# Two layers of an encoder as one block, with the seam between them, the launch and the last store rewritten

## The chip, the cores and the metric

The kernel runs on one core of a Trainium2 chip. The metric is the device time of one execution in microseconds. TensorE (PE) multiplies, VectorE (DVE) and ScalarE (ACT) do the elementwise work, GpSimd (POOL) and SyncE (SP) mostly issue transfers.

## The reference, cut to what matters

Two sequences (256 and 512 tokens, width 1024, float32) pass through the same two layers. They are held together as 768 tokens, six tiles of 128. A layer is:

```
xn   = rms_norm(x, norm1_g)
proj = xn @ w_in          # 9616 columns: q/k/v of A (3 groups x 6 heads x 64),
                          # conv/v/o/gates of B, q/k/v of C, 3 x 1024 branch gates
A: dilated window attention, q and k normed per head and rotated, 3 groups merged
B: bidirectional mLSTM, 4 heads of 128
C: differential attention, 4 heads
x  = x + (sigmoid(g0)*yA + sigmoid(g1)*yB + sigmoid(g2)*yC) @ w_out
hg, hu = rms_norm(x, norm2_g) @ w_ffn_in          # 2 x 2816 columns
x  = x + (silu(hg) * hu) @ w_ffn_out
```

Every product is made of three passes: weights and activations are split into a high part (rounded to the matmul's format) and the low rest, and high x high, high x low and low x high are added up.

## The kernel before, in words

**Programs.** Each engine has its own instruction stream, and they meet on semaphores. There are three blocks. A small first one has SP load x tile 0 and the identity (L712, L713), POOL the other five x tiles, the rotary table and the masks (L717 to L721), and VectorE set `eps`. Then `nc.Fori(0, DEPTH)` (L727) runs the layer block twice, and after each turn clears all semaphores behind a barrier (L2147 to L2151), so that waits can count from zero. The last block stores y in two transfers (L2156, L2157). Every block ends with a barrier of all engines.

**Order in the layer block.** A list, STEPS (`schedule()`, L339), is walked by every engine, each doing its part of each step: `rms` (the square sum and root on ScalarE, then the scaled row on VectorE), `norm` (eight transposes on TensorE, the high copy `xh` on ScalarE, the low rest `xl` on VectorE), `first` (splits of the first eight weight sub-blocks), `piece c t` (chunk c of w_in times token tile t, 24 matmuls, three banks of PSUM in turn), and behind them the steps of attention, mLSTM, gates and branches. In-order engines make this list the order of all work.

**Weights.** SP loads sub-blocks of up to 512 KB into a ring of three (`wraw`, RAW = 3); a load waits on `w_lo`, the count of splits that VectorE has finished. ScalarE makes `wh` from it (L1139, L1368), VectorE `wl` (L1428, L1769). `wh` and `wl` have two halves of four sub-blocks, one per chunk in turn. SPLITS (L420) hangs the splits of chunk c on the steps of chunk c-1 that come after chunk c-2 is done. For chunk 2 these are only the two pieces (1,4) and (1,5), since chunks 0 and 1 are mixed tile by tile (L342 to L344).

**Pieces of A.** The nine chunks 0 to 8 are Q, K, V of group 0, then of groups 1 and 2. A Q or K piece is in HEADS: ScalarE squares it into `stage` (L1189), VectorE sums per head (L1462), ScalarE takes the root, VectorE scales, applies the gain and rotates (L1469 to L1481), and POOL stores the slot (L867). A V piece is in PLAIN: one ScalarE copy (L1196), then the store. POOL takes the stores in the order of STEPS. The first A loads (`load_prep`, L940) come behind piece (3,1), and TensorE's first `a_fold` (L1938) needs them.

**Seam.** SP begins a layer with the gain row (`wide`, L779), two `a_gain` rows, and subs 0 to 3; before sub 4 it copies x to DRAM (L807, 3 MB), before sub 8 it issues nine small loads.

**FFN.** Eleven groups of two tiles of 128 columns. `pe_in` makes a group's two tiles (96 matmuls of 384 columns per tile pair), `silu` turns them into `oh`, `ol`, and `pe_out` multiplies by w_ffn_out: twelve outputs q (tile q // 2, half q % 2) of six matmuls each in eight PSUM banks, each added to x by VectorE (L1820). The last two are called "before last" and "last"; between them nothing is left for ScalarE but the splits of their own weights.

Of the kernel before, what the change touches and what calls it, by code (L numbers as in the profile page):

```python
# [93 lines left out]
FFN_SUB0 = FIRST_SUB[-1]  # L94
WOUT = [(3, 0), (4, 0), (3, 1), (4, 1), (5, 0), (5, 1), (0, 0), (0, 1), (1, 0), (2, 0), (1, 1), (2, 1)]
# [243 lines left out]
def schedule():  # L339
    steps = [("rms", 0), ("first", 0), ("first", 1), ("rms", 1), ("first", 2), ("first", 3), ("norm", 0), ("rms", 2),  # L340
             ("first", 4), ("first", 5), ("norm", 1), ("rms", 3), ("first", 6), ("first", 7)]
# [58 lines left out]
STEPS = schedule()  # L400

# [14 lines left out]
    s[1] % 3 < 2 if s[1] < 9 else s[1] in (C_C, C_C + 1))])}  # L416
# [36 lines left out]
def build(nc, io):  # L453
    ctx = ExitStack()
    with ctx:
# [3 lines left out]
        def sem(name):  # L459
            s = ctx.enter_context(nc.semaphore(name))  # L460
            sems.append(s)
            return s

        sems = []
# [212 lines left out]
        def flip_bank_free(eng, step):  # L677

            before = [s[0] for s in FLIP_BANK[:FLIP_BANK.index(step)]]
            if "c_fold" in before:  # L680
                eng.wait_ge(c_qkt, before.count("c_fold"))
            if "c_flip" in before:
                eng.wait_ge(c_flo, before.count("c_flip"))
# [5 lines left out]
        def norm_half(m, b):  # L689

            if m < 2 * NT - 2:
                at = 1024 * (m % 2) + 512 * b
# [11 lines left out]
        ident_in = ctx.enter_context(nc.semaphore("ident_in"))  # L704
        tables_in = ctx.enter_context(nc.semaphore("tables_in"))
        x_in = [ctx.enter_context(nc.semaphore(f"x_in{t}")) for t in range(NT)]
        x_rows = [io["x_prompt"][0, t * P:(t + 1) * P, :] if t < SEQS[1][0] else
                  io["x_sample"][0, (t - SEQS[1][0]) * P:(t - SEQS[1][0] + 1) * P, :] for t in range(NT)]
        with nc.Block() as block:
            @block.sync  # L710
# [4 lines left out]
            @block.gpsimd  # L715
            def _(pool):
                for t in range(1, NT):  # L717
                    pool.dma_start(x[:, t, :], x_rows[t]).then_inc(x_in[t], 16)
                    if t == 2:
                        pool.dma_start(rope[:, :, :], io["t_rope"]).then_inc(tables_in, 16)  # L720
                pool.dma_start(masks[:, :, :], io["t_masks"]).then_inc(tables_in, 16)  # L721

            @block.vector
            def _(dve):
                dve.memset(eps[:, :], EPS)

        with nc.Fori(0, DEPTH) as layer:  # L727
            with nc.Block() as block:
                w_of = {
                    "in": io["w_in"].rearrange("l (k p) n -> l p k n", p=P),  # L730
                    "branch": io["w_branch"].rearrange("l (k p) n -> l p k n", p=P),
                    "wout": io["w_out"].rearrange("l (k p) n -> l p k n", p=P),
                }
                w_gu = io["w_ffn_in"].rearrange("l (k p) (u f n) -> l u f p k n", p=P, u=2, n=P)
                w_dn = io["w_ffn_out"].rearrange("l (f p) n -> l f p n", p=P)


                def in_bank(a0, ft):

                    return 4 * ((ft + (a0 + 1 if a0 else 0)) % 2)  # L740

                def out_bank(a0, q):

                    return (in_bank(a0 + 1 if a0 + 1 < GROUPS else 2, 0) + (4 if a0 + 1 == GROUPS else 0) + q) % 8

                def in_sub(a):
                    return FFN_SUB0 + 10 + 6 * (a - 2)

                def out_sub(a):
                    return FFN_SUB0 + 14 + 6 * (a - 1)  # L750

                def ffn(step_in, step_out, eng, tallies=()):

                    step_in(0, 0, FFN_SUB0, 0, "first")
                    step_in(0, 1, FFN_SUB0 + 4, 1, "second")
                    step_out(0, 0, FFN_SUB0 + 8, 0, "body")
                    turns = (GROUPS - 3) // 2
                    before = [t.n for t in tallies]  # L760
                    with eng.Fori(0, turns) as i:
                        for t in tallies:
                            t.base = i * t.per
                        step_in(i, 2, in_sub(2), 0, "body")
                        step_out(i, 1, out_sub(1), 1, "body")
                        step_in(i, 3, in_sub(3), 1, "body")
                        step_out(i, 2, out_sub(2), 0, "body")
                    for t, n in zip(tallies, before):
                        assert t.n - n == t.per, (t.n - n, t.per)
                        t.base, t.n = 0, n + t.per * turns  # L770
                    step_in(0, GROUPS - 1, in_sub(GROUPS - 1), 0, "body")
                    step_out(0, GROUPS - 2, out_sub(GROUPS - 2), 1, "before last")
                    step_out(0, GROUPS - 1, out_sub(GROUPS - 2) + 2, 0, "last")


                @block.sync
                def _(sp):
                    bc = lambda ap: ap.partition_broadcast(P)
                    sp.dma_start(wide[:, :], bc(io["norm1_g"][layer])).then_inc(gain1_in, 16)  # L779

                    sp.dma_start(a_gain[:, 0, :], bc(io["a_qn_g"][layer])).then_inc(a_gain_in, 16)
                    sp.dma_start(a_gain[:, 1, :], bc(io["a_kn_g"][layer])).then_inc(a_gain_in, 16)

                    def small_loads():
# [16 lines left out]
                    for c, (kind, subs) in enumerate(CHUNKS):  # L801
                        if c == 2:
                            small_loads()
                        if c == 1:
                            for t in range(NT):
                                sp.wait_ge(x_in[t], 16)
                            sp.dma_start(x_save.rearrange("(t p) d -> p t d", p=P), x).then_inc(x_saved, 16)  # L807
                        for j, (src, k0, nk, col, w) in enumerate(subs):
                            n = FIRST_SUB[c] + j
                            if n >= RAW:  # L810
                                sp.wait_ge(w_lo, n - RAW + 1)
# [4 lines left out]
                    def sp_in(i, a0, base, par, kind):  # L816
                        for j in range(4):
                            r = (base + j) % RAW
                            sp.wait_ge(w_lo, 12 * i + (base + j - RAW + 1))
# [3 lines left out]
                    def sp_out(i, a0, base, par, kind):  # L823
                        for j in range(2):
                            r = (base + j) % RAW
                            sp.wait_ge(w_lo, 12 * i + (base + j - RAW + 1))
# [3 lines left out]
                    sp.wait_ge(x_saved, 16)  # L830


                @block.gpsimd
                def _(pool):
                    def wait_stage(m):

                        for i in range(SLOTS):
                            cnt = (m + SLOTS - i) // SLOTS
                            if cnt:
                                pool.wait_ge(stored[i], 16 * cnt)  # L840

                    def store_staged(step):
                        m = STAGE[step]
                        slot = stage[:, m % SLOTS, :]
                        if step in HEADS:
                            pool.wait_ge(h_ready, HEADS[step] + 1)
                        else:
                            pool.wait_ge(act_staged, PLAIN[step] + 1)
# [8 lines left out]
                        else:  # L857
                            c, t = step[1:]
                            rows = slice(t * P, (t + 1) * P)
                            if c < 9:  # L860
                                dst, src = qkv_a[rows, c % 3, c // 3, :], slot[:, 0:A_W]
# [19 lines left out]
                    def wait_mix_stored(i):  # L881

                        pool.wait_ge(mix_stored[i % GSLOTS], 16 * (i // GSLOTS + 1))

                    def load_gate(i):

                        _, b, d, q = MIX_LIST[i]
                        if i - GSLOTS >= MIX_LAST:
                            pool.wait_ge(r_lo, i - GSLOTS - MIX_LAST + 1)
                        elif i >= GSLOTS:  # L890
                            wait_mix_stored(i - GSLOTS)
                        elif i == GSLOTS - 1:
                            pool.wait_ge(b_dec, len(B_UNITS))
# [3 lines left out]
                    def load_part(j):  # L897

                        _, b, d, q = MIX_LIST[MIX_LAST + j]
                        if j < 2:  # L900
                            pool.wait_ge(c_tr, len(C_FOLDS))
                        if j >= PSLOTS:
                            pool.wait_ge(mixed, MIX_LAST + j - PSLOTS + 1)
# [4 lines left out]
                    def mix(step):  # L908
                        _, b, d, q = step
                        i = MIXES[step]  # L910
                        if i == MIX_LAST:
                            first_parts(2 * KD)
                            pool.wait_ge(d_done, INDEX["turn", 1, NT - 1] + 1)
                            pool.dma_start(wide[:, :], io["norm2_g"][layer].partition_broadcast(P)
                                           ).then_inc(gain2_in, 16)
                        if b < 2:
                            pool.wait_ge(mixed, i + 1)
# [14 lines left out]
                        if KD <= j < KD + NT:  # L932
                            t = FFN_TILES[j - KD]
                            if j == KD:
                                pool.wait_ge(c_flo, len(C_HEADS))
# [4 lines left out]
                    def load_prep(p):  # L940
                        g, s, tq, tk = PREPS[p]
                        r = p % 3
                        if p == 0:
                            pool.wait_ge(n_xn, NT)
                            pool.wait_ge(x_saved, 16)
                            pool.wait_ge(n_lo, NT)
                        if p >= 3:
                            pool.wait_ge(a_tr, p - 2)
                            pool.wait_ge(a_pv, LAST_USE[p - 3])
# [23 lines left out]
                    def store_unit(u):  # L973
# [4 lines left out]
                        pool.wait_ge(a_ov, u + 1)  # L978
# [4 lines left out]
                    def load_merge(t):  # L983
                        if t == 0:
                            for i in range(2):
                                pool.wait_ge(a_stored[i], 16 * A_STORES[-1][i])
# [1200 lines left out]
```

## Time and profile before

| | us |
|---|---|
| median of 3 runs | 3354.35 (3353.36 to 3357.91) |
| the profiled execution | 3353.53 |
| its span, first to last instruction | 3351.9 |
| TensorE busy | 3170.0 (95%) |
| VectorE, ScalarE, POOL busy | 1541.5, 1186.5, 509.5 |
| mean granted TensorE clock | 0.982 |
| first matmul of layer 0, of layer 1 | 19.45, 1684.95 |
| first matmul of piece (0,0) in layer 0, in layer 1 | 31.64, 1697.14 |

The profile gives, for every instruction, its start and length, and what released an engine that had been idle. Idle time of an engine that is not the bottleneck costs nothing. Matmul ends are modelled: neighbouring matmuls overlap in the listing, so distances between starts are what counts. "L1428" is line 1428 of the kernel before.

### The profile page before, as it was taken

What the parts mean: (1) busy time and instruction counts of PE and PEld (TensorE: products, weight loads), DVE (VectorE), ACT (ScalarE), POOL (GpSimd) and SP (SyncE); (2) the same over time, 40 slices, a digit from 0 to 9 for tenths busy, and PEclk for the clock granted to TensorE, in tenths of its full rate; (3) what the DMA queues carried; (4) which work ended last, traced back from release to release, by engine and by line L of the source; (5) the groups of instructions that cost most, each with busy time, mean ns of one, the idle gap of its engine ahead of it and who ended that gap; (6) DMA issues with size and microseconds to landing.
All of it is one profiled execution on the core that took longest, in us unless ns stands there. A gap on an engine that the chain in (4) does not pass through costs nothing. (4 is left out here: it accounts for less than half of the span.)

```text
span 3351.9 us, 46018 instructions
## 1 busy us (share of the span) xinstructions
PE 3170.0 (95%) x17652; PEld 2906.0 (87%) x17652; DVE 1541.5 (46%) x3149; ACT 1186.5 (35%) x2656; POOL 509.5 (15%) x879
## 2 busy tenths in 40 slices
PE   6899999899989999999978999998999999999998
PEld 6899989688878999999878999887887889999997
DVE  5445226644465343443463452365444653434433
ACT  3234434356543211211143344343665422211210
POOL 0111321222242000000001114212222410000000
PEclk9999999999999999999989999999999999999999
DMA  4334444343375122211033344434433742212211
GB/s 162 108 105 123 135 126 129 124 132 120 111 192 181 56 60 61 75 60 52 32 131 104 107 129 134 134 112 124 144 119 122 183 157 63 72 41 75 75 45 62
DMA packets 273323, 358.65 MB, mean 107 GB/s; under 512 B 27377, under 2 KB 209841, under 8 KB 273129
## 3 DMA queue, kind: packets, MB, share of 16 engines
q1 hardware_dynamic: 213576, 179.41, 18.0%
q0 software_dynamic: 59552, 176.68, 16.9%
q8 instruction: 118, 1.93, 0.2%
q14 instruction: 77, 0.62, 0.1%
HBM read 264.42 MB, written 91.59 MB: 106 GB/s over the span
## 5 line engine op out<-in xcount | busy, mean ns | idle before, releaser
L1833 PE MATMUL ps<-wh,xh 128*128 128x384 f32 (+1 forms) x1440 | 537.1, 373 | 18.6 <-DVE wl L1428 11.9
L1835 PE MATMUL ps<-wh,xl 128*128 128x384 f32 (+1 forms) x1440 | 521.2, 362 | 0.0
L1834 PE MATMUL ps<-wl,xh 128*128 128x384 f32 (+1 forms) x1440 | 521.1, 362 | 0.0
L1833 PE MATMUL ps<-xh,wh 128*128 128x384 f32 (+1 forms) x1312 | 459.0, 350 | 12.3 <-issue 7.1
L1428 DVE TENSOR_TENSOR wl<-wraw,wh 128x1024 fp32r<-128x1024 f32 (+2 forms) x210 | 232.5, 1112 | 460.5 <-ACT wh L1139 460.2
L1835 PE MATMUL ps<-xh,wl 128*128 128x384 f32 (+1 forms) x1312 | 443.3, 338 | 0.0
L1834 PE MATMUL ps<-xl,wh 128*128 128x384 f32 (+1 forms) x1312 | 443.0, 338 | 0.0
L1907 PE MATMUL ps<-xl,wh 128*128 128x384 f32 x1280 | 325.0, 334 | 0.0
L1907 PE MATMUL ps<-xh,wl 128*128 128x384 f32 x1280 | 324.9, 334 | 0.0
L1907 PE MATMUL ps<-xh,wh 128*128 128x384 f32 x1280 | 324.7, 334 | 0.0
L1833 PEld LDWEIGHTS ps<-wh,xh 128*128 128x128 f32 x1440 | 277.0, 192 | 51.1 <-DVE wl L1428 13.3
L1835 PEld LDWEIGHTS ps<-wh,xl 128*128 128x128 f32 x1440 | 275.7, 191 | 24.1
L1834 PEld LDWEIGHTS ps<-wl,xh 128*128 128x128 f32 x1440 | 276.8, 192 | 22.1
L1793 DVE SCALAR_TENSOR_TENSOR arena<-arena,ps 128x768 f32<-128x768 f32 x44 | 42.0, 954 | 546.1 <-ACT arena L1390 546.1
L1833 PEld LDWEIGHTS ps<-xh,wh 128*128 128x128 f32 (+1 forms) x1312 | 246.5, 188 | 22.5 <-issue 12.3
L1834 PEld LDWEIGHTS ps<-xl,wh 128*128 128x128 f32 (+1 forms) x1312 | 246.7, 188 | 6.3 <-issue 3.8
L1835 PEld LDWEIGHTS ps<-xh,wl 128*128 128x128 f32 (+1 forms) x1312 | 246.4, 188 | 2.5
L1835 PE MATMUL ps<-wh,ol 128*128 128x512 f32 x624 | 243.2, 390 | 0.0
L1834 PE MATMUL ps<-wl,oh 128*128 128x512 f32 x624 | 243.1, 390 | 0.0
L1833 PE MATMUL ps<-wh,oh 128*128 128x512 f32 x624 | 242.7, 389 | 0.0
L867 POOL DMA_DIRECT2D qkv_a<-stage x108 | 59.0, 546 | 1195.1 <-DVE stage L1481 1051.1
L1390 ACT ACTIVATE arena<-ps 128x768 f32<-128x768 f32 x44 | 35.8, 815 | 560.0 <-PE ps L1907 534.3
(229 smaller groups left out, 5207.4 us busy)
## 6 DMA issues: line engine op xcount, KB each, us to landing
wraw<-in_w_in SPq DMA_DIRECT2D x96, 512.0 KB, 3.8
wraw<-in_w_ffn_in SPq DMA_DIRECT2D x88, 512.0 KB, 4.0
wraw<-in_w_in SPq DMA_DIRECT2D x72, 384.0 KB, 3.6
wraw<-in_w_ffn_out SPq DMA_DIRECT2D x44, 512.0 KB, 3.3
qkv_a<-stage POOLq DMA_DIRECT2D x108, 192.0 KB, 2.2
gate_t<-stage POOLq DMA_DIRECT2D x96, 192.0 KB, 2.2
stage<-gate_t POOLq DMA_DIRECT2D x78, 192.0 KB, 4.3
mix_t<-stage POOLq DMA_DIRECT2D x52, 192.0 KB, 3.8
```

The source lines that it names most:

```text
L867: pool.dma_start(dst, src).then_inc(stored[m % SLOTS], 16)
L1390: act.activation(f_e[:, ft, :].rearrange("p (h n) -> p h n", h=2), ps[:, bank:bank + 2, 0:HALF_TOK], ACT.Tanh, scale=0.5).then_inc(f_ex, 1)
L1428: dve.tensor_tensor(wl[:, half, j, 0:w], wraw[:, n % RAW, 0:w], wh[:, half, j, 0:w].bitcast(F32), ALU.subtract).then_inc(w_lo, 1)
L1793: fch.link(dve.scalar_tensor_tensor(e2, e2, 1.0, ps[:, bank:bank + 2, 0:HALF_TOK], ALU.add, ALU.mult))
L1833: pe.matmul(out, ah, bh, start=first, stop=False)
L1834: pe.matmul(out, ah, bl, start=False, stop=False)
L1835: return pe.matmul(out, al, bh, start=False, stop=last)
L1907: mm = pe.matmul(pair[0:cols, q, 0:HALF_TOK], w[:, half, j, sl_], v[:, k, q * HALF_TOK:(q + 1) * HALF_TOK], start=(k == 0 and w is wh and ...
```

## The change

1. One block for everything. The loop over the layers is written out in Python, so both layers are straight code (the inner loops of the FFN stay). The semaphores are no longer cleared: `past(layer, sem)` adds what one layer counts, from a table PER_LAYER, to every wait of layer 1. The first and the last block go into this one: SP's and POOL's first loads stand at the head of their streams, and `eps` gets a semaphore.
2. The head of STEPS becomes FIRST_STEPS (layer 0 only) and NEXT_STEPS (layer 1). Layer 1's subs 0 to 3 are split, and its norms of tiles 0 and 1 begun, in layer 0's last two FFN groups. The last group's own weights go to half 1, places 2 and 3, so that half 0 is free.
3. Chunk 0's six pieces come first, then chunk 1's; within a group of A the order is V, Q, K (`A_PART`). The norms 2 to 5 stand between the pieces of chunk 0.
4. The `a_gain` rows and the small loads come before sub 4, the copy of x before sub 8. The transposed norms use PSUM banks 4 to 7.
5. y is stored tile by tile, each behind its two last adds.

Cut to its core ("..." where lines are left out):

```diff
+A_PART = (2, 0, 1)
...
-        for part in range(3):
+        for part in A_PART:
...
-    for t in range(4):
-        steps += [("piece", 0, t), ("norm", t + 2)] + ([("rms", t + 4)] if t < 2 else []) + [("piece", 1, t)]
-    steps += [("piece", 0, 4), ("piece", 0, 5), ("piece", 1, 4), ("piece", 1, 5)]
+    steps = [("piece", 0, 0), ("first", 4), ("norm", 2), ("rms", 4), ("piece", 0, 1), ("first", 5), ("norm", 3), ("rms", 5),
+             ("piece", 0, 2), ("first", 6), ("norm", 4), ("piece", 0, 3), ("first", 7), ("norm", 5), ("piece", 0, 4),
+             ("piece", 0, 5)]
+    steps += [("piece", 1, t) for t in range(NT)]
...
+FIRST_STEPS = [("rms", 0), ("first", 0), ("first", 1), ("rms", 1), ("first", 2), ("first", 3), ("norm", 0), ("rms", 2),
+               ("norm", 1), ("rms", 3)]
+NEXT_STEPS = [("norm", 0), ("rms", 2), ("norm", 1), ("rms", 3)]
...
-        with nc.Fori(0, DEPTH) as layer:
-            with nc.Block() as block:
...
+                for layer in range(DEPTH):
...
+                    if layer:
+                        sp.wait_ge(n_lo, past(layer, n_lo))
                     sp.dma_start(wide[:, :], bc(io["norm1_g"][layer])).then_inc(gain1_in, 16)
...
+                            if layer:
+                                sp.wait_ge(f_add, past(layer, f_add))
                             sp.dma_start(x_save.rearrange("(t p) d -> p t d", p=P), x).then_inc(x_saved, 16)
...
+                            if layer and n < RAW:
+                                sp.wait_ge(w_lo, past(layer, w_lo) - (ALL_SUBS - 1 - n) % RAW)
...
+                for t in range(NT):
+                    sp.wait_ge(f_add, past(DEPTH, f_add) - 12 + 2 * t + 2)
+                    y, row = (io["y_prompt"], t * P) if t < SEQS[1][0] else (io["y_sample"], (t - SEQS[1][0]) * P)
+                    sp.dma_start(y[0, row:row + P, :], x[:, t, :]).then_inc(y_out, 16)
...
 ScalarE, act_out:
+                        elif kind == "before last":
+                            for j in range(2):
+                                f_split(i, base + 2 + j, 1, 2 + j)
+                            if layer + 1 < DEPTH:
+                                nc.scalar.preload_act_table_set("natural_log_exp_and_others")
+                                for n in range(4):
+                                    split(0, n, layer + 1)
+                        elif layer + 1 < DEPTH:
+                            rms(0, layer + 1)
+                            rms(1, layer + 1)
...
 VectorE, dve_out, behind the add of q:
+                            if layer + 1 < DEPTH:
+                                if (kind, q) in FIRST_AT:
+                                    split(0, FIRST_AT[kind, q], layer + 1)
+                                if (kind, q) in RMS_AT:
+                                    rms(RMS_AT[kind, q], layer + 1)
+                    FIRST_AT = {("before last", 6): 0, ("before last", 8): 1, ("before last", 10): 2, ("last", 1): 3}
+                    RMS_AT = {("last", 6): 0, ("last", 9): 1}
...
 TensorE, pe_out, behind the matmuls of q:
+                            if kind == "last" and layer + 1 < DEPTH and q in (9, 11):
+                                norm(q // 2 - 4, layer + 1)
...
-            nc.gpsimd.dma_reset()
...
-            nc.gpsimd.sem_clear(range(first, first + len(sems)))
-            nc.all_engine_barrier()
-
-        with nc.Block() as block:
-            @block.sync
-            def _(sp):
-                sp.dma_start(io["y_prompt"].rearrange("b (t p) d -> p (b t) d", p=P), x[:, 0:2, :]).then_inc(y_out, 16)
-                sp.dma_start(io["y_sample"].rearrange("b (t p) d -> p (b t) d", p=P), x[:, 2:NT, :]
-                             ).then_inc(y_out, 16)
```

## Rows read from the trace of the kernel before

**Rows 1.** The page, busy time of each engine.
```profile
PE 3170.0 (95%) x17652; PEld 2906.0 (87%) x17652; DVE 1541.5 (46%) x3149; ACT 1186.5 (35%) x2656; POOL 509.5 (15%) x879
```

**Rows 2.** Stretches: us, busy PE, PEld, DVE, ACT, POOL, PEclk, DMA share, GB/s.
```profile
1127.00:1673.00 546.00, 546.00 (x2908) 514.71 (x2907) 217.88 (x264) 100.98 (x111) 0.00 (x0) 1.00 0.19 57
1673.40:1684.90 11.50, 0.01 (x1) 0.00 (x0) 1.98 (x2) 2.93 (x5) 0.00 (x0) 0.67 0.22 65
1697.10:1756.50 59.40, 56.13 (x320) 55.06 (x320) 41.14 (x91) 24.95 (x59) 5.81 (x11) 0.97 0.33 109
1762.60:1766.10 3.50, 3.47 (x12) 3.11 (x11) 0.34 (x1) 0.72 (x2) 0.00 (x0) 0.52 0.78 218
```

**Rows 3.** Timeline between the layers: start, us, engine, line [idle before <-releaser].
```profile
1646.54 1.22 DVE L1769 TENSOR_TENSOR wl<-wraw,wh 128x1024 fp32r<-128x1024 f32 x1
...
1673.45 0.69 DVE L1820 TENSOR_TENSOR arena<-ps,arena 128x512 f32<-128x512 f32 x1 [0.67 <-PE ps L1835]
...
1679.52 1.28 ACT L1131 ACT_TABLE_LOAD   x1 [33.18 <-issue]
...
1697.14 0.69 PE L1833 MATMUL ps<-wh,xh 128*128 128x384 f32 x1 [1.83 <-DVE xl L1447]
```

**Rows 4.** Timeline of ScalarE, squares of two Q/K pieces in a row.
```profile
1743.83 0.49 ACT L1189 ACTIVATE stage<-ps 128x384 f32<-128x384 f32 x1 [2.51 <-PE ps L1835]
...
1747.99 0.49 ACT L1189 ACTIVATE stage<-ps 128x384 f32<-128x384 f32 x1 [2.51 <-PE ps L1835]
```

**Rows 5.** The chain that ended last: start, us, what.
```profile
1676.10 3.35 issue
...
1716.10 0.87 PE ps L1922 x8
```

**Rows 6.** Timeline of TensorE, beginning of chunk 2 in layer 1.
```profile
1756.82 0.41 PE L1833 MATMUL ps<-wh,xh 128*128 128x384 f32 x1 [0.61 <-DVE wl L1428]
...
1761.51 0.44 PE L1833 MATMUL ps<-wh,xh 128*128 128x384 f32 x1 [2.34 <-DVE wl L1428]
```

**Rows 7.** Timeline around the first A loads of layer 1.
```profile
1798.85 0.54 POOL L867 DMA_DIRECT2D qkv_a<-stage  x1 [3.55 <-DVE stage L1481]
...
1804.80 1.54 PE L1938 MATMUL ps<-ident,arena 128*128 128x128 f32 x6 [10.00 <-DMA arena<-qkv_a]
```

**Rows 8.** Timeline of the launch and of chunk 2's beginning in layer 0.
```profile
4.70 0.54 POOL L721 DMA_DIRECT2D masks<-in_t_masks  x1
...
14.00 1.28 ACT L1131 ACT_TABLE_LOAD   x1 [14.00 <-PEq L709]
...
15.73 9.59 SPq L812 DMA_DIRECT2D wraw<-in_w_in  x4
...
22.96 0.84 ACT L1139 ACTIVATE wh<-wraw 128x768 fp32r<-128x768 f32 x1 [5.96 <-DMA wraw<-in_w_in]
...
31.64 0.69 PE L1833 MATMUL ps<-wh,xh 128*128 128x384 f32 x1 [1.85 <-DVE xl L1447]
...
92.94 0.41 PE L1833 MATMUL ps<-wh,xh 128*128 128x384 f32 x1 [0.60 <-DVE wl L1428]
```

**Rows 9.** DMA issues: queue, count, size of each, median us from issue to landing.
```profile
masks<-in_t_masks POOLq DMA_DIRECT2D x1, 512.0 KB, 8.7
...
arena<-in_x_prompt SPq DMA_DIRECT2D x1, 512.0 KB, 3.6
...
out_y_sample<-arena SPq DMA_DIRECT2D x1, 2048.0 KB, 8.8
```

**Rows 10.** Timeline of the end.
```profile
3339.55 0.69 DVE L1820 TENSOR_TENSOR arena<-ps,arena 128x512 f32<-128x512 f32 x1 [0.67 <-PE ps L1835]
...
3342.69 0.46 SPq L2157 DMA_DIRECT2D out_y_sample<-arena  x1
```

**Rows 11.** Queue 8, 0 to 1676 and 1676 to 3352 us: packets, MB, share.
```profile
q8 instruction: 58, 0.95, 0.2%
...
q8 instruction: 60, 0.98, 0.3%
```

More of the change, by code:

```diff
@@ L727, in build @@
-        with nc.Fori(0, DEPTH) as layer:
-            with nc.Block() as block:
[L729 to L773, printed above, removed]
-                @block.sync
-                def _(sp):
@@ L1115, in _ @@
                             load_turn(*step[1:])
-                    for sem_, total in [(a_loaded[i], loads[i]) for i in range(3)] + [
+                    for sem_, total in [] if layer + 1 < DEPTH else [(a_loaded[i], loads[i]) for i in range(3)] + [
                             (m_loaded[0], NT // 2), (m_loaded[1], NT // 2), (bg_in, 4),
@@ L1425, in split, with _ @@
+                    ffn(act_in, act_out, act)
+            @block.vector
+            def _(dve):
+                dve.memset(eps[:, :], EPS).then_inc(eps_set, 1)
+                chain = Tally(dve, dve_c)
+                fch = Tally(dve, f_ch)
+                fch.per = 2 * 2
+                for layer in range(DEPTH):
+                    def split(c, n, layer=layer):
                         half, j = c % 2, n - FIRST_SUB[c]
                         w = CHUNKS[c][1][j][2] * CHUNKS[c][1][j][4]
-                        dve.wait_ge(w_hi, n + 1)
+                        dve.wait_ge(w_hi, past(layer, w_hi) + n + 1)
@@ L1456, in normed_heads @@
                         i, m = HEADS[step], STAGE[step]
-                        w, gain, q_k = (A_W, a_gain, c % 3) if c < 9 else (C_W, c_gain, c - C_C)
+                        w, gain, q_k = (A_W, a_gain, A_PART[c % 3]) if c < 9 else (C_W, c_gain, c - C_C)
                         n = w // HD
@@ L1814, in dve_out @@
                     def dve_out(i, a0, base, par, kind):
-                        splits = {"body": 4, "before last": 2, "last": 0}[kind]
                         for q in range(12):
@@ L1818, in dve_out, with _ @@
                             xx = x[:, t, h * 512:(h + 1) * 512]
[L1819 removed]
+                            dve.wait_ge(f_out, past(layer, f_out) + 24 * i + (12 * a0 + q + 1))
                             dve.tensor_tensor(xx, ps[:, out_bank(a0, q), :], xx, ALU.add).then_inc(f_add, 1)
[L1821 removed]
+                            if kind == "body" and q % 2 and q // 2 < 4:
                                 f_split(i, base + 2 + q // 2, 0, q // 2)
[L1824 to L1830 removed]
+                            if kind == "before last" and q % 2 and q // 2 < 2:
+                                f_split(i, base + 2 + q // 2, 1, 2 + q // 2)
+                            if layer + 1 < DEPTH:
[5 more added lines that the diff above has]
+                    RMS_AT = {("last", 6): 0, ("last", 9): 1}
+                    ffn(dve_in, dve_out, dve, (fch,))
+                    if layer + 1 == DEPTH:
+                        dve.wait_ge(f_add, past(DEPTH, f_add))
+            @block.tensor
+            def _(pe):
+                for layer in range(DEPTH):
                     def product(out, ah, al, bh, bl, first, last):
@@ L2083, in side_step @@
                             mm.then_inc(c_fl, 1)
-                    for step in STEPS:
+                    for step in ([] if layer else FIRST_STEPS) + STEPS:
                         if step[0] == "norm":
@@ L2109, in first_in @@
                             if q:
[L2110 removed]
+                                pe.wait_ge(n_lo, past(layer, n_lo) + 2 * NT)
                     def pe_in(i, a0, base, par, kind):
@@ L2127, in pe_out @@
                     def pe_out(i, a0, base, par, kind):
-                        half = 0 if kind == "last" else 1
-                        pe.wait_ge(f_lo, 4 * i + (2 * a0 + 2))
+                        first = 2 if kind == "last" else 0
+                        pe.wait_ge(f_lo, past(layer, f_lo) + 4 * i + (2 * a0 + 2))
                         for q in range(12):
```

549 lines of the change are left out of this document (297 added, 252 removed).

## The prediction

> **What bounds the kernel now.** I read the page first, then the stretches, then the timeline at the places where TensorE stops. The page shows TensorE busy 3170 of 3351.9 us, VectorE at 46% and ScalarE at 35% [rows 1]: TensorE sets the time, and what can be won is its idle time and its time at half clock. In the FFN, 1127 to 1673 us, it is busy for all 546.0 us at clock 1.00 [rows 2], so nothing is won or lost there. The idle time lies around the layer starts. Between the last FFN matmul of layer 0 and the first dense one of layer 1, TensorE works 0.01 of 11.5 us [rows 2]; the first matmul of piece (0,0) comes at 1697.14 [rows 3], and the two pieces' 59.4 us that follow hold 56.1 us of busy time, some of it at half clock [rows 2]. The launch has the same shape: nothing dense before 31.64 us [rows 8]. The reader is to see both as one chain: barrier, gain and x, norm, weights split, transposed norm, first piece.
>
> The profiled execution took 3353.53 us for a span of 3351.9; 1.6 us lie outside and stay. The median is 3354.35, 0.8 above it. I sum against 3353.53.
>
> **Layer boundary.** Removed: the end of the block, the clearing of the semaphores, the barrier and the jump back. The last VectorE add ends at 1674.14 and ScalarE's table load starts at 1679.52 [rows 3], 5.4 us. Behind it come the gain row, the first weights and the norms, and the first piece starts at 1697.14 [rows 3]. All of this moves under the last two FFN groups. With one q (6 matmuls, one add) per 1.36 us, 0.69 of add and 0.67 of waiting on VectorE [rows 3], the group "before last" ends at 1657.1 and "last" at 1673.4.
> Sub 0 of the next layer is asked for when the second sub of "before last" has been split, before 1640; subs 1 and 2 when the two last FFN subs are (1647.8, from the split of 1.22 at 1646.54 [rows 3], and 1650.1); sub 3 when sub 0 is (about 1652.9). At 3.6 us each they land by 1657, before VectorE wants sub 3 after q 1 of "last" (1660.5). ScalarE has little else there. VectorE gets four splits of 0.96 us and two norms of 1.28, 6.4 us beside adds of 0.69 per 1.36 us, so it holds 0.67 us free per q over 24 q. TensorE needs an add only 8 q (10.9 us) later: covered. If a weight came more than 10 us late, the in-order VectorE would hold the adds and TensorE with them.
> On TensorE norm 0 goes behind q 9 (0.87 us warm [rows 5]) and norm 1 behind q 11: q 11 ends at 1674.3, norm 1 at 1675.2. VectorE adds q 11 until 1675.1 and makes the low half of norm 0 by 1676.4 (1.23 us). So TensorE idles 1.2 us and piece (0,0) starts at 1676.4. Every later norm is behind a piece: n_lo 3 at 1684.3 for piece (0,2) at 1686.6, n_lo 4 at 1689.4 for 1690.8, n_lo 5 at 1694.4 for 1695.9. The tightest margin is 1.4 us, because the V piece first leaves VectorE free of the head norms.
> Two chunks of pieces are 12 x 4.16 us (the distance of two copies, 1743.83 to 1747.99 [rows 4]) = 49.9, and four norms x 0.87 = 3.5. Chunk 2 can start at 1676.4 + 53.4 = 1729.8. Before, TensorE came to it at 1756.2 (its first matmul at 1756.82 after 0.61 of waiting [rows 6]). **Gain 26.4 us.** Ends: 20 if half the margins above fail, 28 if the 1.2 us go too.
> SP issues the small loads before sub 4 and the copy of x behind sub 7, at about 1683 and not before sub 4. What it then holds up is sub 8, wanted only at about 1705. POOL's first A load waits for that copy, 70 us later: nothing.
>
> **Weights of chunk 2.** Before, its four splits hang on two steps at the end of chunk 1, and TensorE waits 0.61 and 2.34 us [rows 6]. Now chunk 1 follows chunk 0, so they are spread over its six pieces, 12 us and more ahead. Both layers have the stall: 2 x 2.95 = 5.9. In layer 1 the granted clock is 0.52, the level of 1.2 GHz for nearly all of it, in the 3.5 us behind it: 12 matmuls start where 20 fit [rows 2], 1.7 us. **Gain 7.6** (5 to 8).
>
> **V first.** The first A loads follow piece (3,1) in POOL's order. Before, that is a Q piece: POOL stores it at 1798.85, 4.05 us behind the last matmul (1804.80 less the wait of 10.00) [rows 7], after square, sum, root, scale and rotation. Now it is a V piece, one ScalarE pass of 0.49 us (as the square of that size [rows 4]), stored at about +0.7. What follows (memset, loads, 4.1 us of landing) stays: TensorE's wait shrinks from 10.0 to 6.6. The K piece (2,5) now has the head chain, 8 us earlier: its store lands 1.5 us before it is looked for. Chunks 5 and 8 take over the head norms of 3 and 6, and chunks 4 and 7 have these beside attention now without a wait of that kind. **Gain 2 x 3.4 = 6.8** (4 to 9; TensorE's slow clock behind the wait may shrink as well, taken at nothing).
>
> **Launch.** The engines waited at the end of the small first block until the x and mask transfers had landed: the masks are issued at 4.70, land 8.7 us later, and the table load follows at 14.00 [rows 8, 9]. That barrier goes. SP issues wide and subs 0 to 2 from about 1.9 us on, not at 15.73 [rows 8], and the a_gain rows (256 B packets) no longer stand ahead of them. But now x's other five tiles and the masks, 3 MB on POOL's queue, move at the same time. From the landing of sub 0 (22.96) to piece (0,0) (31.64) it was 8.7 us [rows 8]. Lower end: sub 0 lands 3.6 us after its issue at 2.4, 6.0, and piece (0,0) starts at 14.7. Upper end: the weights wait for all of POOL's transfers (13.4), and it starts at 24. I take 19.5, between the ends: SP's three subs and wide, 1.7 MB, share with the 3 MB, sub 0 lands at about 10 and sub 3 at about 17. Gain 12.1 (7.6 to 17).
> The Trainium skill, DMA: Bandwidth & Descriptors, section Queues, rings and completion order, has each DMA engine take turns between the queues, a packet at a time. No row here shows two full queues sharing, so it decides nothing; by it the weights (smaller rows) would get the smaller share, and the start would lie, by my estimate, at 20 to 22.
> Then the two chunks: before 92.34 - 31.64 = 60.7 [rows 8]; now 53.4 plus 1.9, half of the slow first 3.8 us of TensorE, = 55.3. The eleven small loads now stand ahead of sub 4, which ScalarE must have before norm 2; they may hold piece (0,2): 1 us taken (0 to 4). Gain 4.4. **Together 16.5** (8 to 22).
>
> **End.** The last add ends at 3340.24, SP issues y_sample at 3342.69, and it lands 8.8 us later [rows 9, 10]. Now the tiles leave as they are finished, 2.7 us apart, and only the last 512 KB remain: issued at 3340.4, some 3.6 us (as x's tile of that size [rows 9]), end at 3344.6. **Gain 7.3** (5 to 8).
>
> **Sum.** 26.4 + 7.6 + 6.8 + 16.5 + 7.3 = 64.6; 3353.5 - 64.6 = 3288.9, that is 3289 to 3290 beside the median.
>
> **The rivals.**
> *The launch gives back.* Weights queue behind x and the small loads behind them: start at 24, 4 us more in piece (0,2), and V's gain halved: 3300. For it: the transfers of the first 14 us are what the barrier waited for. Against: x's first tile is alone on SP's queue.
> *The boundary stays partly serial.* If ScalarE or VectorE reaches the next layer's norms only behind the last add (a weight late, an in-order wait), then rms, norm and copies for tiles 0 and 1, all of the 12 us before 1697.14, stand open again with 4 of transfer wait and 3 of half clock: 3289 + 19 = 3308. Against: all conditions lie 2 to 10 us ahead of their use.
> *Slower: code.* The second layer's instructions are no longer the first's, fetched in straight line. The one place where fetching shows is the jump (3.35 us of nothing from 1676.10 on [rows 5]). If a block of code stopped TensorE so in the straight line, at 3.35 us each, 20 blocks would eat the gain; with one in two of the 118 fetches of queue 8 [rows 11] it would be 3289 + 59 x 3.35 = 3487. Against: those fetches are there now, 58 in the first half of the span and 60 in the second [rows 11], and TensorE runs 546 us without a gap through some of them. The Trainium skill, Runtime: NRT & Kernel Launch, section Instruction fetch mechanics, says that straight code is fetched ahead and that a taken branch breaks this; by that rule this rival costs nothing.
> *More than forecast.* Other short waits also go (clock behind the A load, start at 15): 3276.
>
> **How the numbers follow.** Forecast 0.66, launch 0.14, boundary 0.10, more 0.05, code 0.03; 0.02 for the change doing none of this. Measurement can tell 0.2%, 6.7 us, from no change. Faster 0.95, same 0.01, slower 0.04. The terms' own ends sum to 3274 to 3311; not all go one way, and with the first two rivals I take 3276 to 3306.
>
> **What would show it.** Right: no table load, no gap above 2 us between the last FFN matmul of layer 0 and chunk 2 of layer 1, 56 us apart; clock 1.00 there; piece (0,0) at 19 to 20 us; no wait at chunk 2; a wait of 6.6 at the first A fold; y's last transfer ending 4.5 us behind the last add. Wrong: a gap behind q 11, adds of the last two groups that fall behind, piece (0,0) later than 24 us, or FFN stretches above 546 us.

## The result, and the profile after

The changed kernel takes 3302.57 us (median of 4 runs, 3299.86 to 3304.63); the kernel before took 3356.13 in the runs beside it. The ratio is 0.9841, 95% interval 0.9824 to 0.9858: 53.6 us faster. The forecast was 3289 with a range of 3276 to 3306. Direction and range hold; the gain is 11 us smaller than the sum of 64.6.

The profiled execution took 3301.47 us for a span of 3299.7, 52.2 less than that of before. The page has TensorE busy as long as before, to 2 us ([rows 1]); what went is nearly all idle time.

```profile
PE 3167.9 (96%) x17652; PEld 2907.4 (88%) x17652; DVE 1541.9 (47%) x3149; ACT 1186.1 (36%) x2656; POOL 509.4 (15%) x879
...
q8 instruction: 116, 1.90, 0.2%
```

The stretches around the boundary (columns as in [rows 2]): the FFN, the last two q with the two transposed norms, and chunks 0 and 1 of layer 1.

```profile
1127.00:1654.00 527.00, 527.00 (x2799) 496.37 (x2798) 217.99 (x262) 105.50 (x119) 0.00 (x0) 1.00 0.22 66
1654.52:1660.20 5.68, 4.65 (x29) 3.88 (x27) 4.44 (x6) 3.55 (x7) 0.00 (x0) 1.00 0.00 0
1660.26:1713.80 53.54, 53.54 (x320) 53.41 (x321) 29.48 (x52) 22.07 (x45) 5.41 (x10) 1.00 0.42 148
```

The reader is to see that the two pieces' chunks, 59.4 us with slow matmuls before, are now 53.54 us of which TensorE is busy for all 53.54, at granted clock 1.00. The timeline at the seam, which answers to [rows 3]: no table load, no pause, TensorE idle for 1.09 us.

```profile
1654.52 1.04 PE L1989 MATMUL ps<-ident,arena 128*128 128x128 f32 x8
...
1658.14 1.03 PE L1989 MATMUL ps<-ident,arena 128*128 128x128 f32 x8
1658.34 0.69 DVE L1872 TENSOR_TENSOR arena<-ps,arena 128x512 f32<-128x512 f32 x1 [0.67 <-PE ps L1898]
1658.94 1.21 DVE L1500 TENSOR_TENSOR xl<-ps,xh 128x1024 fp32r<-128x1024 f32 x1
...
1660.26 0.41 PE L1896 MATMUL ps<-wh,xh 128*128 128x384 f32 x1 [1.09 <-issue]
```

The launch, which answers to [rows 8]: the gain row lands at 8.51, weight piece 0 at 11.84, piece 1 at 15.47, and piece (0,0) starts at 22.16, not at 31.64.

```profile
8.51 1.28 DVE L1491 SCALAR_TENSOR_TENSOR arena<-arena,norm_s,wide 128x1024 f32<-128x1024 f32 x1 [7.62 <-DMA wide<-in_norm_g]
...
11.84 0.84 ACT L1176 ACTIVATE wh<-wraw 128x768 fp32r<-128x768 f32 x1 [5.24 <-DMA wraw<-in_w_in]
...
15.47 0.84 ACT L1176 ACTIVATE wh<-wraw 128x768 fp32r<-128x768 f32 x1 [2.80 <-DMA wraw<-in_w_in]
...
22.16 0.69 PE L1896 MATMUL ps<-wh,xh 128*128 128x384 f32 x1 [0.90 <-DVE xl L1500]
```

The first A loads, against [rows 7]: POOL stores the V piece at once, and TensorE waits 7.27 us in both layers, not 9.87 and 10.00.

```profile
112.21 0.54 POOL L900 DMA_DIRECT2D qkv_a<-stage  x1 [3.62 <-ACT stage L1236]
...
118.60 1.11 PE L2005 MATMUL ps<-ident,arena 128*128 128x128 f32 x4 [7.27 <-DMA arena<-qkv_a]
...
1754.55 1.33 PE L2005 MATMUL ps<-ident,arena 128*128 128x128 f32 x5 [7.27 <-DMA arena<-qkv_a]
```

The new loss stands in the attention stage, ahead of TensorE's fourteenth `a_turn` (the step that transposes the six blocks of probabilities of one unit of attention, counted from 0, so number 13). Piece (8,3) is now a K piece:

```profile
313.23 0.55 DVE L1515 TENSOR_REDUCE head_s<-stage 128x6 f32<-128x384 f32 x1 [1.68 <-ACT stage L1229]
...
316.28 1.22 DVE L1481 TENSOR_TENSOR wl<-wraw,wh 128x1024 fp32r<-128x1024 f32 x1
...
317.42 0.28 DVE L1595 CUSTOM_DVE_ANT_0 arena<-ps,masks 128x128 f32<-128x128 f32 x1
...
317.75 0.40 ACT L1278 ACTIVATE arena<-arena 128x128 f32<-128x128 f32 x1 [2.44 <-DVE arena L1595]
...
320.21 1.49 PE L2028 MATMUL ps<-ident,arena 128*128 128x128 f32 x6 [2.35 <-ACT arena L1278]
```

VectorE works through the head chain from 313.23 on, then a weight split of 1.22 us, and only then comes to the six score maxima; the six exponentials on ScalarE follow one by one to 320.07, and TensorE, which has nothing else in its order, waits 2.35 us. Its six transposes then take 1.49 us: half clock. In the kernel before, with a V piece there, the same step waited 0.26 us and took 0.87:

```profile
339.48 0.87 PE L1961 MATMUL ps<-ident,arena 128*128 128x128 f32 x6 [0.26 <-ACT arena L1238]
```

Each matmul of one trace set against the same matmul of the other gives the account of the 52.2 us. In chunks 0 and 1 the order differs, so there only the ends are compared:

| part | forecast | measured | from |
|---|---|---|---|
| launch, to the start of chunk 2 | 16.5 | 14.5 | 92.34 to 77.85 |
| weights of chunk 2 | 7.6 | 8.8 | 3.7 and 5.1 in the two layers |
| V first, the wait at the A fold | 6.8 | 5.3 | 2.6 and 2.7 |
| V first, slow clock behind it | 0 | 4.7 | 2.1 and 2.6 |
| V first, chunks 5 to 8 and the first gates | 0 | -12.2 | -6.8 (0.9 of it at the gates) and -5.4 |
| boundary | 26.4 | 26.4 | saving at the last FFN matmul 16.0, at chunk 2's start 42.4 |
| end | 7.3 | 8.6 | behind the last matmul |
| all else | 0 | -3.8 | nearly all in the second half of layer 1 |

Of the last row, 3.3 us lie at one place, in the stage of C of layer 1. TensorE waits there for four loads of `qkv_c`; first the kernel before, then the changed one:

```profile
2488.17 0.66 PE L2036 MATMUL ps<-ident,arena 128*128 128x128 f32 x4 [0.95 <-DMA arena<-qkv_c]
```
```profile
2442.88 0.66 PE L2103 MATMUL ps<-ident,arena 128*128 128x128 f32 x4 [2.67 <-DMA arena<-qkv_c]
```

In both, POOL issues the first load 4.5 us ahead of the last matmul before the wait. The loads land 5.1 us after their issue (median) in one and 6.7 us in the other, and in the 4.5 us behind the wait the granted clock is 1.00 in one and 0.62 in the other. The DMA view from the first issue to the end of the wait (2482.40 to 2488.17 before, 2435.38 to 2442.88 after) has an instruction fetch in the changed kernel alone:

```profile
q8 instruction: 1, 0.02, 1.9%
```

The other traces say the same. In the changed kernel and its ten variants a fetch of 16 KB begins between the issues and the landings, and the last three loads take 5.9 to 6.8 us; in the kernel before and in e7 it begins behind the wait, and they take 4.8 to 5.1. At the same place of layer 0 no trace has a fetch there, and they take 4.6 to 5.7. So the fetch goes with the late loads in all 26 cases. That it causes them isn't shown: no run moves a fetch.

### The profile page after: what moved, and what is told of

Read it like the earlier page. It is cut to its first block, busy times and chain, and to the rows that moved or that the text cites. A ratio compares the mean times of both kernels' runs of the same rounds, so it can differ in the third digit from the quotient of the medians.

```text
span 3299.7 us, 45375 instructions
## 1 busy us (share of the span) xinstructions
PE 3167.9 (96%) x17652; PEld 2907.4 (88%) x17652; DVE 1541.9 (47%) x3149; ACT 1186.1 (36%) x2656; POOL 509.4 (15%) x879
## 4 chain that ended last, share of the span: by engine, by line
PE 77%; DVE 9%; ACT 5%; issue 4%; DMA 3%; POOL 2%; SPq 0%; ACTq 0%; POOLq 0%; DVEq 0%
PE ps L1972 20%; PE ps L1896 16%; PE ps L1898 16%; PE ps L1897 16%; PE ps L2043 1%; PE ps L2117 1%; PE ps L2091 1%; PE ps L2028 1%; DVE wl L1481 1%; PE ps L2005 1%; PE ps L2017 1%; ACT arena L1278 1%; DVE stage L1525 1%; DVE stage L1522 1%; PE ps L2139 1%
```

## The experiments

Theory: the forecast's sum is right but for V first, whose last chunk of each group, now K, gives back in chunks 5 to 8 what it gains at the A fold; and at the launch the two DMA queues share. Rivals: V first is a pure gain and the stage lost its time to something else; the launch hangs on the engines' order; the boundary's gain is all interleaving. Times are medians; ratios are against the kernel before, run beside each. The experiments ran in three sets, and the median of the kernel before lay between 3355.05 and 3358.60 in them, so a difference between medians of two sets is good to about 3 us, and one between ratios or traces is better.

**Q first everywhere.** (e1)
```
-A_PART = (2, 0, 1)
+A_PARTS = ((0, 1, 2), (0, 1, 2), (0, 1, 2))      # by group
```


> The changed kernel with the pieces of all three head groups in the order Q, K, V as before the change; all else as changed. Theory (K last costs in the attention stage): the first A fold waits 10 us again instead of 7.6, and the half clock behind it grows back, 4.5 us a layer lost; in chunks 5 to 8 about 6 us a layer come back, the 2.66 us gap behind a_turn 13 among them. Net 3300, between 3296 and 3304, and the matmul times of the attention stage run parallel to the kernel before. Rival (V first is a pure gain, the stage lost its time to something else in the change): 3302.6 + 9 = 3312, and the 2.66 us gap stays.


Measured 3306.88, ratio 0.9854 [0.9839, 0.9869]; profiled 3305.41. The first fold waits 10.29 us again:
```profile
125.86 1.54 PE L2010 MATMUL ps<-ident,arena 128*128 128x128 f32 x6 [10.29 <-DMA arena<-qkv_a]
```
The wait at a_turn 13 is back at 0.26 us in both layers; here layer 1, and then the stretch around it in layer 0:
```profile
1962.77 0.87 PE L2033 MATMUL ps<-ident,arena 128*128 128x128 f32 x6 [0.26 <-ACT arena L1283]
```
```profile
300.00:345.00 45.00, 44.52 (x298) 43.08 (x296) 13.34 (x54) 18.82 (x55) 11.14 (x19) 1.00 0.51 150
```
The changed kernel has in the same stretch:
```profile
300.00:345.00 45.00, 42.17 (x273) 40.47 (x272) 23.88 (x85) 19.16 (x62) 9.35 (x16) 0.96 0.47 137
```
TensorE 44.52 us busy against 42.17, VectorE 13.34 against 23.88. Matmul by matmul against the changed kernel, the order Q, K, V loses 5.0 and 4.5 us at the fold of the two layers and has 5.9 and 4.4 back by chunk 9. So the rival falls. The time is still 3 us above the theory's bound: another 4.2 us go at the launch and 3.5 at the boundary, where chunk 0 now has head norms beside the last norms of x. The theory had left that out.

**V first in groups 0 and 1 alone.** (e2)
```
+A_PARTS = ((2, 0, 1), (2, 0, 1), (0, 1, 2))
```


> The changed kernel with V, Q, K in groups 0 and 1 and Q, K, V in group 2. Theory: the gap behind piece (8,4) and the slow clock after it go (4.4 us a layer) and the small one at the first gates (0.7); the shorter wait at the first A fold stays: 3302.6 - 10 = 3293, the 1.4 us around piece (5,4) stay as well. Rival (the gap is not the K piece's head chain): 3302, gap of 2.66 us unchanged.


Measured 3294.58, ratio 0.9814 [0.9801, 0.9828]: as the theory has it. The split stands ahead of the maxima as before, but VectorE had been free for 8.66 us:
```profile
315.68 1.23 DVE L1486 TENSOR_TENSOR wl<-wraw,wh 128x1024 fp32r<-128x1024 f32 x1 [8.66 <-ACT wh L1181]
316.82 0.28 DVE L1600 CUSTOM_DVE_ANT_0 arena<-ps,masks 128x128 f32<-128x128 f32 x1
...
319.63 0.87 PE L2033 MATMUL ps<-ident,arena 128*128 128x128 f32 x6 [0.26 <-ACT arena L1283]
```
The wait is 0.26 instead of 2.35 us, and the transposes take 0.87 instead of 1.49.

**V first in group 1 alone.** (e3)
```
+A_PARTS = ((0, 1, 2), (2, 0, 1), (0, 1, 2))
```


> The changed kernel with V, Q, K in group 1 alone, so that only the chunk that the first A loads follow is V. Theory: the A fold's wait stays at 7.6 us as in the changed kernel, since it is piece (3,1) that counts; the head norms of chunk 0 stand beside the last norms at each layer's start and cost 0 to 2 us each: 3293 to 3297. Rival: the V chunk at the layer's start is what keeps the start free of gaps; then 4 us a layer are lost there: 3301.


Measured 3300.11, ratio 0.9832 [0.9818, 0.9845]: outside the theory's 3293 to 3297 and near the rival's 3301. Both had a part of it. Most of the fold's gain stays with piece (3,1) alone (waits of 8.02 and 8.12 us, against 7.85 and 7.40 in e2 and 10.29 in e1), but head norms in chunk 0 cost 3.9 us at the launch and 3.5 at the boundary, matmul by matmul, so V first in group 0 pays for itself there.

**Q, V, K in group 2.** (e11)
```
+A_PARTS = ((2, 0, 1), (2, 0, 1), (0, 2, 1))
```


> V, Q, K in groups 0 and 1 as in e2_v_in_two, but Q, V, K in group 2: V in the middle, K still last. Theory (what counts is that chunk 8 is one with head norms when the last a_turn of its stretch comes, not where V stands else): the gap of 2.66 us behind a_turn 13 and its slow clock are back, 3302 (a little under the changed kernel at most). Rival (V ahead of Q and K in group 2 is what costs): as e2_v_in_two, 3294.


Measured 3301.54, ratio 0.9834 [0.9821, 0.9847], 7 us above e2. The wait is back in both layers, so it is the K chunk in last place that costs:
```profile
320.39 1.54 PE L2033 MATMUL ps<-ident,arena 128*128 128x128 f32 x6 [2.34 <-ACT arena L1283]
```

**V first alone, in the kernel before.** (e7)
```
-        for part in range(3):
+        for part in (2, 0, 1):      # and the places that map a chunk to its part
```


> The kernel before with one part of the change alone: the pieces of each head group in the order V, Q, K. Theory (the shorter A fold wait and the slow clock behind it, 4.5 us a layer, are eaten by the K pieces' head chain in chunks 5 and 8, 5 to 6 us a layer): 3356.5 with a spread of 3353 to 3360, and the 2.66 us gap behind a_turn 13 is there. Rival (the forecast's own term holds where the rest of the change is absent): 3356.5 - 7 = 3349.5 or less, no such gap.


Measured 3361.82 (11 runs, 3354.88 to 3365.82), ratio 1.0020 [1.0010, 1.0029]: by itself this part is slower, and above the expected spread of 3353 to 3360. In the profile the matmuls run 6.0 us ahead of the kernel before behind the first fold and only 0.3 us ahead at the start of chunk 9 of layer 0 (6.1 and 0.5 in layer 1), with the same wait:
```profile
336.89 1.26 PE L1962 MATMUL ps<-ident,arena 128*128 128x128 f32 x6 [2.34 <-ACT arena L1239]
```
The profiled run (3354.88) is the fastest of the eleven and fits the theory; the median lies 7 us above it. That rest isn't explained.

**x held at the launch.** (e4)
```
+                    if t == 2:
+                        pool.wait_ge(w_in_s[1], 16)
                     pool.dma_start(x[:, t, :], x_rows[t])
```


> The changed kernel, but x's tiles 2 to 5, the rope table and the masks are asked for only when the second weight piece has landed. Theory (at the launch the two queues share, and x's 3 MB slow the weights): sub 0 lands at about 8 us instead of 11.8, piece (0,0) starts at 18 to 19 instead of 22.2, and the time is 3299; tile 2 lands by 15, before its norm wants it. Rival (sharing does not matter, the start hangs on the order on ScalarE and VectorE): 22 us again and 3302.6, or slower if tile 2 comes late and piece (0,2) waits for it.


Measured 3297.47, ratio 0.9824 [0.9811, 0.9838], and piece (0,0) at 18.16:
```profile
9.07 0.84 ACT L1178 ACTIVATE wh<-wraw 128x768 fp32r<-128x768 f32 x1 [2.66 <-DMA wraw<-in_w_in]
...
10.40 0.54 POOL L864 DMA_DIRECT2D arena<-in_x_sample  x1 [8.47 <-DMA wraw<-in_w_in]
...
18.16 0.69 PE L1898 MATMUL ps<-wh,xh 128*128 128x384 f32 x1 [2.25 <-DVE xl L1502]
```
The DMA view of 2 to 12 us (packets, MB, share): first the changed kernel, then this one.
```profile
q0 software_dynamic: 560, 2.00, 51.6%
q1 hardware_dynamic: 771, 1.56, 46.1%
```
```profile
q1 hardware_dynamic: 1242, 2.27, 66.3%
q0 software_dynamic: 157, 0.58, 14.9%
```
The queue of the weights, q1 (x's first tile and the gain row too), moves 2.27 instead of 1.56 MB in that time. The sharing theory holds, for 4 us at the launch.

**Small loads later.** (e9)
```
-                        if c == 1:
-                            small_loads()
+                            if (c, j) == (1, 3):
+                                small_loads()
```


> The changed kernel, with the eleven small loads of each layer issued ahead of the last weight piece of chunk 1 instead of ahead of its first. Theory (piece (0,0) at 22 us leaves the fifth weight piece time enough, so the 1 us that the forecast charged for them was not there): 3302.6, no difference. Rival (they slow the launch): 1 to 3 us faster.


Measured 3304.75, ratio 0.9838 [0.9824, 0.9851]: no difference that the runs can tell, so the 1 us charged for them wasn't there.

**The boundary's norms and splits behind the FFN.** (e5)
```
-                            if layer + 1 < DEPTH:      # in dve_out; likewise in act_out and pe_out
-                                if (kind, q) in FIRST_AT: ...
-                                if (kind, q) in RMS_AT: ...
-                    for step in (NEXT_STEPS if layer else FIRST_STEPS) + STEPS:
+                    for step in FIRST_STEPS + STEPS:
```


> The changed kernel with one part of the boundary undone: there is still one block without barrier or clearing, and the next layer's gain row and first weights are still asked for in the last FFN groups, but VectorE's norms and splits and TensorE's first two transposed norms come behind the last FFN group, in the launch's order. Theory (barrier and late transfers were the larger part of the 27 us, the interleaving the smaller): behind the last add stand 1.28 + 2 x 0.96 + 1.28 + 2 x 0.96 + 1.23 us and the landing of sub 3 asked for only then, so piece (0,0) starts about 9 us behind the last add instead of 1 to 2, 2 us of half clock follow: 3302.6 + 9 = 3311.6, between 3309 and 3315. Rival (the interleaving brings nearly all of it): 3302.6 + 19 or more, 3322.


Measured 3309.92, ratio 0.9862 [0.9846, 0.9877], 7.4 us above the changed kernel (8.5 at the boundary in the traces).
```profile
1659.80 0.69 DVE L1867 TENSOR_TENSOR arena<-ps,arena 128x512 f32<-128x512 f32 x1 [0.67 <-PE ps L1888]
1660.40 1.28 DVE L1486 SCALAR_TENSOR_TENSOR arena<-arena,norm_s,wide 128x1024 f32<-128x1024 f32 x1
...
1665.82 0.84 ACT L1176 ACTIVATE wh<-wraw 128x768 fp32r<-128x768 f32 x1 [13.38 <-DMA wraw<-in_w_in]
...
1668.93 0.66 PE L1886 MATMUL ps<-wh,xh 128*128 128x384 f32 x1 [2.23 <-issue]
```
Piece (0,0) starts 8.4 us behind the last add, not 1.2, at half clock (0.66 and then 0.52 us a matmul). So of the boundary's 26.4 us some 8 are the interleaving, and 3.5 are V first in chunk 0 (e1, e3). The rest, by difference, is the dropped barrier, reset, table load and the gain row and first weights that are there in time; these weren't run one by one.

**All of y behind the last add.** (e6)
```
-                    sp.wait_ge(f_add, past(DEPTH, f_add) - 12 + 2 * t + 2)
+                    sp.wait_ge(f_add, past(DEPTH, f_add))
```


> The changed kernel, but all six y transfers wait for the last add. Theory (the end's gain is the 2.5 MB that leave earlier): the last landing moves from about 3 to about 11 us behind the last add, 3302.6 + 8 = 3310.6. Rival (the gain at the end came from the dropped end of the block): 3303 to 3305.


Measured 3308.99, ratio 0.9863 [0.9848, 0.9878], 6.4 us above the changed kernel (6.6 in the traces, behind the last matmul). So about 6.5 of the end's 8.6 us are the early tiles; the other 2 fit the 2.4 us that lay between the last add and the issue of y_sample in [rows 10].

**Towards a better version.** e8 joins V first in two groups and the held x, and at the launch puts norm 0 ahead of the third split, with norm 1 behind piece (0,0):
```
-FIRST_STEPS = [rms 0, first 0, first 1, rms 1, first 2, first 3, norm 0, rms 2, norm 1, rms 3]
+FIRST_STEPS = [rms 0, first 0, first 1, norm 0, first 2, rms 1, first 3, rms 2, norm 1, rms 3]
+FIRST_PE = [norm 0, piece (0,0), norm 1]
```


> V, Q, K in groups 0 and 1 and Q, K, V in group 2; x's tiles 2 to 5 and the masks held until the second weight piece has landed; and at the launch the copies of norm 0 stand ahead of the third and fourth splits, with norm 1 behind piece (0,0) on TensorE. Theory: the first two add up, 8 + 5 us below the changed kernel, and piece (0,0) starts at about 14 us instead of 18.5, 4 us more: 3302.6 - 17 = 3285.5. Rival (the early start only moves the wait to the third and fourth weight pieces or to norm 2): 3290, with gaps inside piece (0,0) or ahead of piece (0,2).


Measured 3290.17, ratio 0.9805 [0.9791, 0.9818]. The rival is nearer: piece (0,0) starts at 13.85, but TensorE then waits for norm 1 and norm 2, the latter behind a split whose weight lands at 27.57, with the small loads ahead of it on SP. Behind chunk 1, e8 is 3.7 us ahead of the changed kernel, no more than e4 with its 4.0: the earlier norm 0 earned nothing there.
```profile
13.85 0.69 PE L1904 MATMUL ps<-wh,xh 128*128 128x384 f32 x1 [2.37 <-DVE xl L1508]
...
24.24 0.44 PE L1904 MATMUL ps<-wh,xh 128*128 128x384 f32 x1 [1.50 <-DVE xl L1508]
...
27.57 0.85 ACT L1184 ACTIVATE wh<-wraw 128x768 fp32r<-128x768 f32 x1 [2.66 <-DMA wraw<-in_w_in]
...
30.64 0.45 PE L1904 MATMUL ps<-wh,xh 128*128 128x384 f32 x1 [1.10 <-DVE xl L1508]
```
The last one, e10, moves the small loads, as in e9, on top of that:


> The kernel of e8_best with the small loads issued ahead of the last weight piece of chunk 1. Theory (the early start now waits for the fifth weight piece, which stands behind the small loads on SP: it landed at 27.6 us): norm 2 is no longer held by it, the 1.3 us gap and the slow clock around it go, 3 to 4 us: 3290.2 - 3.5 = 3286.7. Rival (the transfers of x, masks and weights share the time to 30 us in any order): 3290, with the wait moved to norm 3.


Measured 3290.59, ratio 0.9792 [0.9779, 0.9806]. The wait at norm 2 is gone (the split starts at 24.55, and behind chunk 1 its profile is 1.6 us ahead of that of e8), but the two versions can't be told apart by time. Both beat the changed kernel and the one before: 0.9792 has an interval wholly below that of 0.9841.

## Why the prediction was right, and where not

**Boundary: right in cause and size.** 26.4 us forecast and measured; the trace has the forecast's order: q 11, norm 1, VectorE's low half, 1.1 us idle, no gap in the two chunks. The adds kept pace. That V in chunk 0 keeps VectorE free there, the forecast's ground for its tightest margin, is borne out: with Q there 3.5 us are lost (e1, e3). The price of the serial rival was far too high: with norms and splits behind the last add the time was 7.4 us worse, not 19: the stretch from last add to first piece was 8.4 us, not 12 and 4 more, and 2.2 us of slow clock followed, not 3.

**Weights of chunk 2: right**, 8.8 against 7.6: the waits were 3.2 a layer, and half clock behind them took 0.5 and 1.9 more, where the forecast had 1.7 in one layer.

**V first: the failed step.** It was put as "Chunks 5 and 8 take over the head norms of 3 and 6, and chunks 4 and 7 have these beside attention now without a wait of that kind." For chunk 8 that is wrong, and its price was put at nothing: the chain of (8,3), 3.1 us on VectorE from the sum to the rotation, and a split of 1.22 us stand ahead of the maxima of one unit, and TensorE's order leaves it nothing to do meanwhile. That K in the last place does it is shown (e2 takes the wait away, e11 brings it back; e2 is 8.0 us faster than the changed kernel). The step judged a place by what its neighbours cost instead of by the slack at that place: in e2's trace the split finds VectorE idle for 8.66 us and the wait is 0.26, so the cover was nearly used up already. The smaller losses of the stage, 1.4 us about piece (5,4) and 0.9 at the first gates of layer 0, weren't tested one by one. On the other side the term was too small: the fold's wait shrank by 2.6 and 2.7 in the two layers, not by 3.4, but 4.7 us of half clock behind it went too, taken at nothing. Sum of the three: -2.2 instead of +6.8; and in the launch and the boundary V first earns 7.4 to 7.7 us more (e3, e1), which the forecast held inside those terms.

**Launch: right in kind, 2 us short.** Piece (0,0) starts at 22.16, not at 19.5, and chunks 0 and 1 take 55.7 us against 55.3 forecast. Between 8 and 16 us, with both queues full, q0 moves 639 packets and 2.25 MB, q1 642 packets and 0.94 MB: the same number of packets, not of bytes. The Trainium skill, DMA: Bandwidth & Descriptors, section Queues, rings and completion order, has each engine take turns between the queues by the packet; the trace agrees as far as its equal counts of packets show it. The start that the prediction worked out by that rule, 20 to 22, was nearer than the 19.5 taken.

**End: right**, 8.6 against 7.3, since a tile lands 2.6 us after its issue, not 3.6.

**The slower rival, code.** As it was put, it didn't happen: the instruction queue makes 116 fetches against 118, TensorE is busy for 527.00 of 527.00 us in the FFN and for all of the 53.54 us behind the seam, and the price of 3.35 us a fetch didn't show anywhere. What the forecast had not thought of is a fetch that falls among loads which TensorE is about to need. The 3.3 us at `qkv_c` in layer 1 fit that; it is argued from traces, not tested.

**All else.** The other 0.5 us of that row is the rest of differences that go both ways, by 1 to 2 us, in the second half of layer 1; they weren't looked into.

**The range.** At its low end the terms' own ends sum to 3353.5 - 75 = 3278.5, not to 3274; the range's 3276 came from a rival, so nothing hangs on it. That 3302.57 lies inside is owed to the width of the range: V first came out 9 us lower, the launch 2 and all else 3.8, against 2.5 more from the weights and the end. The rivals at 3300 and 3308 lie nearer in number, but neither is what happened: piece (0,0) started at 22.16 and not at 24, and nothing was serial at the boundary.

## What to carry to other kernels

When work is reordered, each place that receives it needs its own slack worked out: what the in-order engine does just ahead of the result that the bounding engine waits for there. A rotation of equal pieces can gain at one place and lose the same at another; per-group orders then take the gain without the loss, here 8 us. When a barrier is dropped, the transfers behind it and ahead of it start together, and here the two queues then moved equal numbers of packets: hold back what isn't wanted first (4 us in e4).

## What the runs showed of the hardware that was not expected

A short wait of TensorE can cost about twice its length. At a_turn 13 a wait of 2.35 instead of 0.26 us was followed by transposes at 1.49 us instead of 0.87, and the granted clock in 300 to 345 us was 0.96 against 1.00. Matmul by matmul the place cost 4.4 us: 2.1 of wait, 1.7 of half clock (1.2 instead of 2.4 GHz) behind it, 0.6 at the next unit's transposes. At the first fold, a wait 2.6 to 2.7 us shorter saved another 2.1 and 2.6 us of half clock behind it.

It need not. In the kernel before, TensorE waits 2.34 us for chunk 2's weights in both layers. In layer 1 the clock behind it was 0.52 ([rows 2, 6]); in layer 0 it was 1.00, and the matmuls behind the first took 0.34 us, as at full clock:
```profile
97.64 0.44 PE L1833 MATMUL ps<-wh,xh 128*128 128x384 f32 x1 [2.34 <-DVE wl L1428]
```
```profile
97.60:101.10 3.50, 3.37 (x18) 3.06 (x19) 0.96 (x1) 1.03 (x3) 0.00 (x0) 1.00 0.69 186
```
So the half clock behind a wait of this length was there in one place and not in the other, and a forecast needs it as a range.

With two queues active, the one whose packets were 1.5 KB on average got 0.94 MB through while the one at 3.5 KB got 2.25 MB, at equal packets (8 to 16 us); issuing most of the second 8 us later let the first carry 45% more (2.27 against 1.56 MB between 2 and 12 us).

Loads that had a 16 KB instruction fetch fall among them landed 5.9 to 6.8 us after their issue, and 4.6 to 5.7 us without one, at the same place of the program in 13 traces. The fetch took 1.2 to 2.2 us.
